# Inverting the delta rule's triangular systems as blocks of 64 rows on GpSimd instead of blocks of 32 with two levels on TensorE

## What is computed

```python
M = jnp.where(strict, jnp.einsum('bhncd,bhnsd->bhncs', kb, k) * decay, 0.0)
T = lax.linalg.triangular_solve(eye + M, jnp.broadcast_to(eye, M.shape),
                                left_side=True, lower=True, unit_diagonal=True)
u = jnp.einsum('bhncs,bhnsd->bhncd', T, v * beta[..., None])
w = jnp.einsum('bhncs,bhnsd->bhncd', T, kb * jnp.exp(G)[..., None])
```

## Time and profile before

| | |
|---|---|
| median of 3 runs | 2070.06 us (2069.72 to 2071.79) |
| the profiled execution | 2070.83 us, its span 2069.0 us |
| TensorE busy | 2036.1 us, 98% |
| VectorE, ScalarE, GpSimd busy | 57%, 30%, 14% |
| mean granted clock of TensorE | 0.998 of full speed |
| chain that ended last | 89% TensorE |
| DMA | 227 MB, mean 110 GB/s |

### The profile page before, as it was taken

How to read it: one execution, slowest core, us unless ns; L and a number is a source line. 1 busy time by engine, 2 the same in 40 slices (tenths; PEclk the granted TensorE clock), 3 DMA queues, 4 the chain that set the end, 5 groups by cost and what they waited for, 6 DMA issues and landing times.

```text
span 2069.0 us, 30409 instructions
## 1 busy us (share of the span) xinstructions
PE 2036.1 (98%) x12940; PEld 1950.6 (94%) x12940; DVE 1176.5 (57%) x1357; ACT 626.1 (30%) x794; POOL 285.5 (14%) x275
## 2 busy tenths in 40 slices
PE   8999999999999999999999999999999999999998
PEld 7999998999999999999999999999999999999996
DVE  6457564666677646566433343466565656565656
ACT  5213334434333544334443332211111111111113
POOL 0000003758280222222000002000000000000002
PEclk9999999999999999999999999999999999999999
DMA  8235567655555755645253211111011101110102
GB/s 281 93 103 134 143 157 205 187 182 162 164 154 133 172 178 135 183 152 151 66 186 108 90 69 51 62 61 52 31 51 51 52 31 51 52 52 31 61 31 82
DMA packets 252204, 227.11 MB, mean 110 GB/s; under 512 B 141102, under 2 KB 209622, under 8 KB 251942
## 3 DMA queue, kind: packets, MB, share of 16 engines
q1 hardware_dynamic: 252070, 225.17, 35.8%
HBM read 161.29 MB, written 63.84 MB: 109 GB/s over the span
## 4 chain that ended last, share of the span: by engine, by line
PE 89%; DVE 4%; ACT 2%; DMA 2%; issue 2%; SPq 1%; POOL 0%; POOLq 0%; DVEq 0%; ACTq 0%
PE a_psum L886 33%; PE a_psum L145 30%; PE a_psum L1155 11%; PE a_psum L873 4%; PE a_psum L961 1%; PE a_psum L979 1%; PE a_psum L1062 1%; PE a_psum L943 1%; PE a_psum L1005 1%; PE a_psum L958 1%; PE a_psum L989 1%; DMA w_raw<-in_w_in 1%; PE a_psum L1077 1%; PE a_psum L1085 1%; PE a_psum L1076 1%
## 5 line engine op out<-in xcount | busy, mean ns | idle before, releaser
L886 PE MATMUL a_psum<-xh,w_hi 128*128 128x348 f32 (+1 forms) x1656 | 536.8, 324 | 2.1 <-DVE w_lo L1505 1.3
L886 PE MATMUL a_psum<-xl,w_hi 128*128 128x348 f32 (+1 forms) x1656 | 531.9, 321 | 0.0
L886 PE MATMUL a_psum<-xh,w_lo 128*128 128x348 f32 (+1 forms) x1656 | 530.2, 320 | 0.0
L886 PEld LDWEIGHTS a_psum<-xh,w_hi 128*128 128x128 f32 x1656 | 311.9, 188 | 5.7 <-DVE w_lo L1505 1.9
L886 PEld LDWEIGHTS a_psum<-xl,w_hi 128*128 128x128 f32 x1656 | 312.3, 189 | 1.0
L886 PEld LDWEIGHTS a_psum<-xh,w_lo 128*128 128x128 f32 x1656 | 312.1, 188 | 0.0
L1283 ACT ACTIVATE post<-a_psum 128x348 f32<-128x348 f32 (+1 forms) x207 | 94.7, 457 | 555.9 <-PE a_psum L886 515.0
L1209 ACT ACTIVATE w_hi<-w_raw 128x1024 fp32r<-128x1024 f32 x125 | 132.0, 1056 | 429.8 <-PE a_psum L145 409.2
L145 PE MATMUL a_psum<-xh,w_hi 128*128 128x342 f32 (+1 forms) x1152 | 244.7, 321 | 9.0 <-DVE xl L1527 9.0
L1505 DVE TENSOR_TENSOR w_lo<-w_raw,w_hi 128x1024 fp32r<-128x1024 f32 x125 | 156.5, 1252 | 158.6 <-ACT w_hi L1209 158.6
L145 PE MATMUL a_psum<-xl,w_hi 128*128 128x342 f32 (+1 forms) x1152 | 244.7, 320 | 0.0
(11 more groups left out here) (239 smaller groups left out, 2806.6 us busy)
## 6 DMA issues: line engine op xcount, KB each, us to landing
w_raw<-in_w_in SPq DMA_DIRECT2D x76, 512.0 KB, 3.7
w_raw<-in_w_up SPq DMA_DIRECT2D x44, 512.0 KB, 3.4
mix_scratch<-post SPq DMA_DIRECT2D x32, 522.0 KB, 2.8
down_raw<-in_w_ffn_down SPq DMA_DIRECT2D x22, 512.0 KB, 4.5
ext<-mix_scratch SPq DMA_DIRECT2D x9, 1024.0 KB, 7.0
y<-mix_scratch SPq DMA_DIRECT2D x18, 512.0 KB, 5.5
ext<-grow_scratch SPq DMA_DIRECT2D x9, 512.0 KB, 5.3
ext<-mix_scratch SPq DMA_DIRECT2D x9, 512.0 KB, 6.5
```

The source lines that it names most:

```text
L886: mm = pe.matmul(psum[:, u % 2, 0:n], w[:, k, :], x[:, k, at0 + n * j:at0 + n * j + n], start=(k == 0 and part == 0), stop=(k == KC - 1 an ...
```

## The change

**Blocks of 64.** GpSimd inverts the two diagonal blocks of 64 x 64 of each head of chunks 1 to 8: 2 x 8 x 8 = 128 systems, one per partition, in one run, in place: M, with its sign turned (VectorE makes MB negative), is overwritten by the inverse without the product for its own column. For j = 1 to 62 a pair of instructions on (63 - j) x j elements. Chunk 0 has 8 systems of 16 rows, on 8 partitions (inv0, 14 pairs). The planned steps for the run begin at u = 46 and end at u = 84; their number per step follows a budget of elements.

**Gathers and placing by loads.** Blocks are no longer compacted by ScalarE and transposed by VectorE. M of each chunk, chunk 0 too, is stored, and mgather(c) on SP waits for that store and loads the blocks with "r h s -> h r s", a system to a partition, in pieces of 256 bytes (two loads a chunk). The inverses are stored as they are (x, 1 MB, for dl_d) and, turned by eight strided copies of 512 elements on GpSimd (xturn, u = 87 to 90) with two buffers, as xt (xstore, u = 88 to 91, 256 KB each). dl_x places them by two loads of 256-byte pieces on the diagonal of dxt, which GpSimd has zeroed once (zero_t). l6r's result is copied as before.

**One level.** l5q, l5r, expand, comp, tin and tout go, and so do the loads of dm5. l6q and l6r stay.

**The order.** mst moves to u = 28, 29, 31, 32, 34, 36, 38, 40 and 42, and dl_x, dl_k and tk in the plan a little.

```diff
-        at = (28, 29, 31, 32, 34, 37, 40, 43, 46)[c]
+        at = (28, 29, 31, 32, 34, 36, 38, 40, 42)[c]
...
+        steps[max(at + 3, 34)].append(("mgather", c))
...
+    steps[35].append(("inv0",))
+    steps[41].append(("x0store",))
+    u, j, room = 46, 1, 0
+    while j < B64 - 1:
+
+        room += 1000 if u < 53 else 1600
+        n = j
+        while n < B64 - 1 and room > 0:
+            room -= n * (B64 - 1 - n) + 270
+            n += 1
+        if n > j:
+            steps[u].append(("inv", j, n))
+        j, u = n, u + 1
+    for n in range(TURNS):
+        steps[87 + n // 2].append(("xturn", n))
+        steps[88 + n // 2].append(("xstore", n))
...
+                        for n in range(2):
+                            part, to = slice(B64 * n, B64 * n + B64), B64 * n + GH * (c - 1)
+                            sp.dma_start(invv[to:to + GH, :, :], sc["m"][c, part, :, part].rearrange("r h s -> h r s")
+                                         ).then_inc(mi_ld, 16)
...
+                    if n == 0:
+                        sp.wait_ge(p_inv, INV_ALL)
+                        sp.dma_start(sc["x"], inv[0:B64, :]).then_inc(x_st, 16)
+                    sp.wait_ge(p_inv, INV_ALL + n + 1)
+                    sp.dma_start(sc["xt"][:, 512 * n:512 * n + 512], xt[n % 2]).then_inc(xt_st[n % 2], 16)
...
+                        sp.dma_start(dxt[c % 2][part, :, part], sc["xt"][at0:at0 + GH, :].rearrange("h (s r) -> s h r", r=B64)
+                                     ).then_inc(xc_ld[c % 2], 16)
...
-                elif kind == "l5q":
-                    c = a[0]
-                    pe.wait_ge(m_ld, 32 * c)
-                    pe.wait_ge(p_exp, 2 * c)
+                elif kind == "l6q":
+                    c = a[0]
+                    pe.wait_ge(m_ld, 16 * c)
+                    pe.wait_ge(xc_ld[c % 2], 32 * ((c + 1) // 2) + (0 if c % 2 else 16))
                     pe.wait_ge(d_attn, 2 * c + 2)
...
+            def invert(x, prod, base, systems, n, j):
+
+                shape = (systems, n - 1 - j, j)
+                prod = prod[:, 0:shape[1] * j].rearrange("p (r s) -> p r s", s=j)
+                pool.wait_ge(p_inv, base + 2 * j - 1)
+                pool.tensor_tensor(prod, x[:, j + 1:n, j:j + 1].broadcast_to(shape), x[:, j:j + 1, 0:j].broadcast_to(shape),
+                                   ALU.mult).then_inc(p_inv, 1)
+                pool.wait_ge(p_inv, base + 2 * j)
+                pool.tensor_tensor(x[:, j + 1:n, 0:j], x[:, j + 1:n, 0:j], prod, ALU.add).then_inc(p_inv, 1)
...
+                    j0, j1 = a
+                    if j0 == 1:
+                        pool.wait_ge(mi_ld, 16 * 2 * (NCH - 1))
+                        pool.memset(inv[:, 0:B64 * B64:B64 + 1], 1.0).then_inc(p_inv, 1)
                     for j in range(j0, j1):
...
+                        invert(invv, prod1, INV_BASE, P, B64, j)
+                elif kind == "xturn":
+                    n = a[0]
+                    pool.wait_ge(p_inv, INV_ALL)
+                    if n >= 2:
+                        pool.wait_ge(xt_st[n % 2], 16 * (n // 2))
```

More of the change, by code:

```diff
@@ L303, in front_plan @@
     add(("dl_v", 0))
+    add(("tk", 0))
     add(("oload", 0))
@@ L321, in front_plan @@
         add(("tr", c))
-        if n:
-            add(("l5q", c + 1))
         fill()
@@ L327, in front_plan @@
             add(("su", c))
-            add(("l5r", c + 1))
         add(("osl", c))
@@ L786, in _ @@
                         sp.wait_ge(kt_st, 16 * 8 * KC)
-                        sp.wait_ge(d_tout, 2 * NBATCH)
+                        sp.wait_ge(x_st, 16)
+                        for n in range(2):
+                            sp.wait_ge(xt_st[n], 16 * TURNS // 2)
                     sp.dma_start(kd[c % 2].rearrange("p h c -> p (h c)"), sc["kt"][c]).then_inc(kd_ld, 16)
```

264 lines of the change are left out of this document (93 added, 171 removed).

## The result

| | before | after |
|---|---|---|
| median | 2070.14 us (2069.72 to 2071.79) | 2128.28 us (2127.15 to 2131.74) |
| ratio, 95% interval | | 1.0277 [1.0264, 1.0289] |
| span of the profiled execution | 2069.0 us | 2126.2 us |
| mean granted clock of TensorE | 0.998 | 0.983 |

A forecast was written before the change was run, and what follows sets the result against it. TensorE, busy 98%, was taken as the bound, with GpSimd a hidden second limit. On 2070.8 us, -17.1 + 23 + 2 + 1 + 1 - 1 = +9 gave 2079.7; with the median 0.8 lower, 2079 us, range 2053 to 2098.

The forecast's parts named there:

- Less TensorE work: Chunks 1 to 8: dropping l5q and l5r removes 16 runs of 1.07 us from TensorE's path, -17.1 us.
- (d): Delta chunks: placed blocks come by a load, not VectorE and ScalarE work; -2 to 0 us, taken as -1.
- GpSimd's price: Inversion run on GpSimd: 62 pairs on 41,664 elements cost 184 us clean, 196 with the upper slope.
- the law: Price of a GpSimd product-and-subtraction pair: 0.55 us fixed plus 3.6 ns per element, from pairs of 31 and 255 elements.
- The start at 419: GpSimd's inversion starts when the last gather, issued behind unit 45 at 413.5, lands 5.3 us later.
- (a): VectorE's convolution instructions delayed by GpSimd's longer ones, making its results late; 0 to 2 us a chunk, 2 in all.
- The +23 for GpSimd: Retention stage: GpSimd's products come late for TensorE's r_out matmuls; the largest lateness, at chunk 7, counts, +23 us.
- VectorE becomes the bound: Rival: VectorE needs 31 us a retention chunk, 39 late plus half the upper slope (6 us); 2099 us, chance 0.14.
- (b): SP's queue: gathers and reordered mst steps among stores freeing rv_stage, 17 more issues and waits; 0 to 5 us, taken as 1.
- (c): Eight turns and 3 MB of stores go ahead of delta-rule chunk 0's loads; -1 to +5 us, taken as 1.
- GpSimd keeps pace: Rival: less contention and a lower slope let TensorE's queue forgive GpSimd's lateness; 2054 us, chance 0.28 including under 10 us late.
- The level's loads: Rival: l6q and l6r matmuls wait for placed blocks loaded in 256-byte pieces; 0 to 1 us a chunk, left in the range.

The follow-up runs named there:

- halves: Changed kernel with every GpSimd product and addition on the 128 systems cut in two by rows; 2129.76 us.
- taps_apart: Changed kernel with diagonal blocks stored in system order, one load replacing chunks 1 to 8's gathers, and each tile's four filter instructions issued two by two, one unit apart; 2103.86 us.
- spread_halves: Changed kernel with inversion instructions on 128 systems cut in two by rows, 1353 elements a step instead of 1600, turns and stores later; 2124.27 us.

## Why the prediction was wrong, step by step

- **Less TensorE work, -17.1, and fewer waits in the delta chunks, -1 (d): right.** From unit 99 to 139 the lag falls by 17.6 us.
- **GpSimd's price: right.** The run starts at 441.11 and its last addition begins at 705.57. Forecast were 263.9 us from the start to the end of the eighth retention product; it ended 270.5 us after the start, 12.5 of it idle for loads. A pair of 992 elements without VectorE beside it took 4.22 us, start to start, and the law gives 4.12:

```profile
563.60 1.91 POOL L1943 TENSOR_TENSOR ext<-ext 128x992 f32<-128x992 f32 x1
565.59 2.15 POOL L1946 TENSOR_TENSOR ext<-ext 128x992 f32<-128x992 f32 x1
567.82 1.91 POOL L1943 TENSOR_TENSOR ext<-ext 128x992 f32<-128x992 f32 x1
```

- **The start at 419: right in TensorE's time** (441.1 less the lag of 21.3 at unit 45 is 419.8).
- **"I take 2 us in all, since GpSimd is later still" (a): this step failed.** It let VectorE's delays disappear under GpSimd's. VectorE's busy share was read (15 us a chunk, up to 28 of 30 under contention), and not where in its queue the burst of five stands: directly ahead of the chain from the output's square to the state. The +23 for GpSimd and +2 for VectorE became 46: 33 us more of idle TensorE, mostly waits for VectorE's state (25.0 of all 36.5), and 14 of matmuls at a lower clock. The mechanism was the rival "VectorE becomes the bound", which had chance 0.14 and a price of 39 for seven chunks, and some 45 with its half slope. Against it I had said that large instructions leave pauses; the taps at 2.55 us say that they don't. Its condition, no idle time left in VectorE, was wrong too: VectorE works 219 of 287 us there. An in-order queue holds its successors long before it is full.
- **"0 to 5 us, I take 1" (b): the largest miss in proportion, 21 us.** I counted issues and waits in SyncE's queue and took the landing time of one load, 5.3 us, from loads of a different shape. What counted was that the sixteen loads each fall on 8 partitions (10.6 us of the 21.6 stay with large pieces) and are cut into 8,192 pieces (the other 11), in the stage in which rv_stage is freed by stores on the same queue.
- **"1 us" (c): 4.4 to unit 103 in the changed kernel, 18 to 24 wherever the turns stand two to four units later.** The mutual wait of turn and store, two buffers deep, was not in the sum; in the changed kernel it cost little.
- **The clock.** The working put the later clock inside GpSimd's lateness. Idle TensorE costs again when it restarts: 13.8 + 7.7 = 21.5 of the 67 us.
- **Rivals.** "GpSimd keeps pace" did not come true: its run takes what was forecast. That TensorE waits for it at one chunk only, 7.0 us, is because VectorE already holds TensorE back; with that wait gone (halves) GpSimd's shows. The level's loads took no place: L1014 waits 7.2 us for mix_scratch, which is no load of the level.

Forecast 2079, measured 2128: of the 49 us between them 20 are in (b), 21 in the retention stage (46 - 25), and some 7 behind it, in (c) and up to unit 103. No repair gives a kernel faster than before. The best complete one, taps_apart, keeps 37.6 us of the retention stage's cost and 2103.9 us in all. Even where both limits were relieved 27 us stayed (spread_halves), more than the 17 that the removed level is worth. What makes up these 27 is open; the run that has them waits 18.8 us for GpSimd's product, 15.6 of it at once, between 500 and 560 us, and no run tried a thinner plan there.

## What to carry to other kernels

Before work is given to an engine that shares a port, look at what stands behind each burst of the other engine in its in-order queue, and price the burst at its length under contention; the engine's busy share says nothing about that. Where two engines' delays lie side by side, take neither as hidden by the other: repair of one shows the other at full size. Lay a gather out so that its outermost dimension is large on both sides, or put the small pieces into the store, and count every pair of waits between a producer and its store as a round trip of the queue.

## What the runs showed of the hardware

- VectorE's two-input instructions of 1,040 elements took 1.30 us beside GpSimd memsets or tiny reads, 1.93 beside halved and 2.55 beside full reading instructions. GpSimd writing only, 170 of 239 us, cost them nothing; an instruction with one input of 1,040 elements took 1.38 beside it and 0.75 beside tiny reads.
- 256-byte pieces written from 64 partitions landed in 2.6 us for 128 KB and cost the stage 2.8 us; 256-byte pieces loaded onto 8 partitions raised the landing of 512 KB stores from 2.9 to 7.1 us, took up to 2.0 us each to issue, and cost 21.6.
- After 10.4 us of idle time TensorE's granted clock was 0.50 from 561.0 to 564.2 us, the lower of its two levels, and eight matmuls took 3.63 instead of 1.89 us.
- GpSimd's slope of 3.6 ns per element for a product and an addition, read from pairs of 31 to 255 elements, held at 992.
